# Two transformer blocks: sums of squares in two rounded parts, and the delta rule's first pair of heads prepared beside the gate projection

## The reference

```python
proj = hn @ w_in
qkv = silu(causal_conv(proj[..., :3 * 1024], w_conv))       # 4 taps, 24 heads' worth of 128 channels
gate = proj[..., 3 * 1024:4 * 1024]
q = l2_norm(q) * 128 ** -0.5;  k = l2_norm(k)               # over each head's 128 channels, 8 + 8 heads
g = -exp(a_log) * softplus(a_in + dt_bias)                  # decays; beta = sigmoid(b_in)
o = gated_delta_rule(q, k, v, g, beta)                      # chunked: a triangular solve per chunk, then a scan
o = rms_norm(o, norm_g) * silu(gate)
...
k = rms_norm(kv[:, :, 0], k_norm);  q = rms_norm(q, q_norm) # the later attention: 8 + 8 heads of 128
```

## Time and profile before

| | |
|---|---|
| three runs | 3090.63, 3101.42 and 3102.06 us, median 3101.42 |
| the profiled execution | 3092.16 us, span on the core 3090.2 us |
| PE busy | 2967.1 us, 96% of the span |
| DVE busy | 1464.2 us, 47% |
| ACT busy | 1074.8 us, 35% |
| POOL busy | 241.5 us, 8% |
| granted TensorE clock, mean | 0.986 of full |
| chain that ended last, share of PE | 81%, with L582 alone 64% |

### The profile page before, as it was taken

How to read it: one execution, slowest core, us unless ns; L and a number is a source line. 1 busy time by engine, 2 the same in 40 slices (tenths; PEclk the granted TensorE clock), 3 DMA queues, 4 the chain that set the end, 5 groups by cost and what they waited for, 6 DMA issues and landing times.

```text
span 3090.2 us, 46737 instructions
## 1 busy us (share of the span) xinstructions
PE 2967.1 (96%) x21198; PEld 2437.0 (79%) x21198; DVE 1464.2 (47%) x1427; ACT 1074.8 (35%) x1169; POOL 241.5 (8%) x136
## 2 busy tenths in 40 slices
PE   8998889999999999999999999999998998999998
PEld 6777767888877878888878887778877887788886
DVE  6655534444353444443354434455567664544432
ACT  4453333222254563222342223342244432232222
POOL 1002101000010001000110000330002211010001
PEclk9999889999999999999999999999999999999999
DMA  3210012222322102223222223312140002222221
GB/s 140 82 58 2 2 36 101 96 96 102 109 98 82 69 28 96 96 96 112 99 96 95 96 97 108 118 49 88 66 141 6 3 5 113 82 96 96 95 102 75
DMA packets 44901, 249.28 MB, mean 81 GB/s; under 512 B 8444, under 2 KB 12284, under 8 KB 17185
## 3 DMA queue, kind: packets, MB, share of 16 engines
q1 hardware_dynamic: 43552, 242.11, 22.1%
q10 hardware_dynamic: 1152, 4.19, 0.3%
HBM read 237.90 MB, written 8.39 MB: 80 GB/s over the span
## 4 chain that ended last, share of the span: by engine, by line
PE 81%; DVE 6%; ACT 3%; issue 2%; POOL 1%; DVEq 0%; ACTq 0%; POOLq 0%
PE ps L582 64%; PE ps L2672 7%; PE ps L1362 2%; PE ps L1990 1%; PE ps L2268 1%; ACT whi L266 1%; PE ps L2252 1%; DVE wlo L272 1%; PE ps L3705 1%; PE ps L3686 0%; PE ps L3717 0%; PE ps L3468 0%; DVE gdn_XX L1704 0%; PE ps L1422 0%; DVE rw_u L1035 0%
## 5 line engine op out<-in xcount | busy, mean ns | idle before, releaser
L272 DVE TENSOR_TENSOR wlo<-wraw,whi 128x2048 fp32r<-128x2048 f32 x210 | 486.6, 2317 | 987.8 <-ACT whi L266 987.7
L266 ACT ACTIVATE whi<-wraw 128x2048 fp32r<-128x2048 f32 x210 | 402.1, 1915 | 968.5 <-PE ps L582 968.4
L582 PE MATMUL ps<-ffn_xh,whi 128*128 128x512 f32 x1408 | 554.2, 394 | 3.6 <-DVE ffn_xl L389 2.1
L582 PE MATMUL ps<-ffn_xh,wlo 128*128 128x512 f32 x1408 | 550.0, 391 | 0.0
L582 PE MATMUL ps<-ffn_xl,whi 128*128 128x512 f32 x1408 | 549.3, 390 | 0.0
L582 PEld LDWEIGHTS ps<-ffn_xh,whi 128*128 128x128 f32 x1408 | 264.9, 188 | 61.1 <-DVE ffn_xl L389 2.5
L582 PEld LDWEIGHTS ps<-ffn_xh,wlo 128*128 128x128 f32 x1408 | 264.5, 188 | 59.2
L582 PEld LDWEIGHTS ps<-ffn_xl,whi 128*128 128x128 f32 x1408 | 264.7, 188 | 56.5 <-issue 0.7
L582 PE MATMUL ps<-ffn_uh,whi 128*128 128x512 f32 x704 | 276.6, 393 | 0.0
L582 PE MATMUL ps<-ffn_uh,wlo 128*128 128x512 f32 x704 | 274.9, 391 | 0.0
L582 PE MATMUL ps<-ffn_ul,whi 128*128 128x512 f32 x704 | 274.7, 390 | 0.0
(11 more groups left out here) (500 smaller groups left out, 4711.6 us busy)
## 6 DMA issues: line engine op xcount, KB each, us to landing
wraw<-in_weights SPq DMA_DIRECT2D x211, 1024.0 KB, 4.7
gates_kept<-gates_tmp ACTq DMA_DIRECT2D x8, 512.0 KB, 4.2
mix_gate<-gates_kept SPq DMA_DIRECT2D x8, 512.0 KB, 10.7
h<-in_x SPq DMA_DIRECT2D x4, 512.0 KB, 8.5
mix_y<-hz_kept SPq DMA_DIRECT2D x2, 1024.0 KB, 5.8
out<-out SPq DMA_DIRECT2D x4, 512.0 KB, 3.2
wraw<-in_weights SPq DMA_DIRECT2D x2, 512.0 KB, 6.9
ple_raw<-in_p SPq DMA_DIRECT2D x4, 256.0 KB, 5.1
```

Of the source, the lines that this page charges most:

```text
L266: c.nc.scalar.activation(c.whi[:, j % 2, :], c.wraw[:, j % 2, :], ACT.Copy).then_inc(c.hi_ready, 1)
L272: c.nc.vector.tensor_tensor(c.wlo[:, j % 2, :], c.wraw[:, j % 2, :], c.whi[:, j % 2, :].bitcast(F32), ALU.subtract).then_inc(c.lo_ready, 1)
L582: last = nc.tensor.matmul(pair[:, m, :], a, b, start=opens and n == 0 and wa + xa == 0, stop=closes and n == len(ks) - 1 and wa == 1)
```

## The change

Three things. First, each pair's squares are no longer summed as float32: ACT rounds them to float32r (`hi`), DVE subtracts (`lo`), and PE sums both parts, each as a float32r matmul; `Scales` and `HeadNorm` both do so, with single buffers `sq`, `hi`, `lo`. Second, in `gdn_qkv` the sum of pair p moves from its place after tile p + 3 to the middle of tile p + 2, and `Scales` comes ahead of `Decays` among the hooks of ACT and DVE. Third, stage -1 of `DeltaCore` is gone: the preparation of pair 0 is issued beside the gate projection's tiles 2 and 3, with buffers and PSUM banks of its own, and the zeroing of `XTf` moves into slot 2 of the first build. The lines of the attributes renamed by this (`self.KB` to `self.KB[p]` and the like) are left out below.

```diff
 class Scales
-        self.sq = [c.at(f"gdn_sq{b}", [P, 2, T], sq_at + 4096 * b) for b in range(4)]
+        self.sq, self.hi, self.lo = (c.at(f"gdn_sq{n}", [P, 2, T], sq_at + 4096 * b, dt)
+                                     for b, (n, dt) in enumerate((("", F32), ("h", F32R), ("l", F32R))))
-        self.hot = c.at("gdn_hot", [P, 2 * HEADS - 1], 20480)
+        self.hot = c.at("gdn_hot", [P, 2 * HEADS - 1], 20480, F32R)
...
     scalar_beside
             act.wait_ge(*self.qkv_part.A.at(f"gdn_qkv.func{p}"))
-            if p >= 4:
-                act.wait_ge(*self.E.at(f"sum{p - 4}"))
-            nc.scalar.activation(self.sq[p % 4][:, :, :], self.qkv[:, 2 * p:2 * p + 2, :], ACT.Square)\
+            if p:
+                act.wait_ge(*self.V.at(f"sqlo{p - 1}"))
+            nc.scalar.activation(self.sq[:, :, :], self.qkv[:, 2 * p:2 * p + 2, :], ACT.Square)\
                 .then_inc(*self.A.done(f"sq{p}"))
+            act.wait_ge(*self.A.at(f"sq{p}"))
+            if p:
+                act.wait_ge(*self.E.at(f"sum{p - 1}"))
+            nc.scalar.activation(self.hi[:, :, :], self.sq[:, :, :], ACT.Copy).then_inc(*self.A.done(f"sqhi{p}"))
...
     vector_beside
         if r == 1:
             nc.vector.memset(self.rows[:, :, :].bitcast(F32), 0.0).then_inc(*self.V.done("rows0"))
             nc.vector.memset(self.one[:, :].bitcast(F32), 0.0).then_inc(*self.V.done("one0"))
+        if 1 <= r <= 8:
+            p = r - 1
+            dve.wait_ge(*self.A.at(f"sqhi{p}"))
+            nc.vector.tensor_tensor(self.lo[:, :, :], self.sq[:, :, :], self.hi[:, :, :].bitcast(F32), ALU.subtract)\
+                .then_inc(*self.V.done(f"sqlo{p}"))
...
+    def tensor_halfway(self, pe, r):
+        nc, c = self.c.nc, self.c
+        if 2 <= r <= 9:
+            p = r - 2
+            pe.wait_ge(*self.V.at(f"sqlo{p}"))
+            for m in range(2):
+                h = 2 * (p % 4) + m
+                for part in (self.hi, self.lo):
+                    last = nc.tensor.matmul(c.ps[0:HEADS, 7 - p // 4, :], self.hot[:, HEADS - 1 - h:2 * HEADS - 1 - h],
+                                            part[:, m, :], start=h == 0 and part is self.hi,
+                                            stop=h == HEADS - 1 and part is self.lo)
+            last.then_inc(*self.E.done(f"sum{p}"))
...
     tensor_beside
-        if 3 <= r <= 10:
-            p = r - 3
-            pe.wait_ge(*self.A.at(f"sq{p}"))
-            pe.wait_ge(*self.V.at("hot"))
-            for m in range(2):
-                h = 2 * (p % 4) + m
-                last = nc.tensor.matmul(c.ps[0:HEADS, 7 - p // 4, :], self.hot[:, HEADS - 1 - h:2 * HEADS - 1 - h],
-                                        self.sq[p % 4][:, m, :], start=h == 0, stop=h == HEADS - 1)
-            last.then_inc(*self.E.done(f"sum{p}"))
 class DeltaCore
-        for s in range(-1, GP + 2):
+        for s in range(GP + 2):
...
     gpsimd
-        pool.wait_ge(self.c.tile_done, self.j_held)
         pool.wait_ge(self.loaded, 48)
         pool.wait_ge(*self.scales.V.at("cols"))
+        pool.wait_ge(*self.scales.A.at("low2"))
         self.pool_mask(pool, 0)
+        pool.wait_ge(self.c.tile_done, self.j_held)
...
     tensor
-        self.misc_read = None
-        pe.wait_ge(*self.scales.V.at("cols"))
-        pe.wait_ge(*self.scales.A.at("low2"))
+        self.misc_read = self.at("kb", 0)
+        pe.wait_ge(*self.gate_part.free(2))
+        pe.wait_ge(*self.gate_part.free(3))
...
+    def tensor_beside(self, pe, r):
+        if r == 2:
+            pe.wait_ge(*self.scales.A.at("low2"))
+            for s in (13, 15, 5):
+                self.pe_prepare(pe, 0, s)
+
+    def tensor_halfway(self, pe, r):
+        if r == 3:
+            pe.wait_ge(*self.scales.V.at("cols"))
+            self.pe_prepare(pe, 0, 7)
+            pe.wait_ge(*self.at("eg", 0))
+            self.pe_prepare(pe, 0, 9)
+            pe.wait_ge(*self.at("eg", 1))
+            self.pe_prepare(pe, 0, 11)
+
+    def single(self, p, s):
+        return self.bank({13: 4, 15: 5, 5: 7, 7: 6, 9: 4, 11: 5}[s] if p == 0 else self.MISC)
...
+    def scalar_early(self, act, r):
+        if r == 3:
+            self.c.nc.scalar.preload_act_table_set(LOG_EXP)
+            for s in (13, 15, 17):
+                self.act_prepare(act, 0, s)
...
+    def vector_beside(self, dve, r):
+        if r == 2:
+            dve.wait_ge(*self.scales.V.at("cols"))
+            for s in (13, 15, 16, 5, 7, 9, 11, 17):
+                self.dve_prepare(dve, 0, s)
...
     dve_build, slot 2
+            if k == 0:
+                nc.vector.memset(self.XTf[HALF:P, :, :, 0:HALF], 0.0).then_inc(*self.done("zero"))
 class HeadNorm
     scalar_beside
             if p:
+                act.wait_ge(*self.V.at(f"sqlo{p - 1}"))
+            nc.scalar.activation(self.sq[:, :, :], self.two(p), ACT.Square).then_inc(*self.A.done(f"sq{p}"))
+            act.wait_ge(*self.A.at(f"sq{p}"))
+            if p:
                 act.wait_ge(*self.E.at(f"sum{p - 1}"))
-            nc.scalar.activation(self.sq[:, :, :], self.two(p), ACT.Square).then_inc(*self.A.done(f"sq{p}"))
+            nc.scalar.activation(self.hi[:, :, :], self.sq[:, :, :], ACT.Copy).then_inc(*self.A.done(f"sqhi{p}"))
...
     vector_beside
+        if 0 <= s - 1 < 8:
+            p = s - 1
+            dve.wait_ge(*self.A.at(f"sqhi{p}"))
+            nc.vector.tensor_tensor(self.lo[:, :, :], self.sq[:, :, :], self.hi[:, :, :].bitcast(F32), ALU.subtract)\
+                .then_inc(*self.V.done(f"sqlo{p}"))
...
     tensor_beside
-            pe.wait_ge(*self.A.at(f"sq{p}"))
+            pe.wait_ge(*self.V.at(f"sqlo{p}"))
             if p:
                 pe.wait_ge(*self.A.at(f"log{p - 1}"))
             for m in range(2):
-                last = c.nc.tensor.matmul(c.ps[:, 6 + m, :], c.ones[:, :], self.sq[:, m, :], start=True, stop=True)
+                for part in (self.hi, self.lo):
+                    last = c.nc.tensor.matmul(c.ps[:, 6 + m, :], c.ones[:, :].bitcast(F32R), part[:, m, :], start=part is self.hi,
+                                              stop=part is self.lo)
 delta_stage
-    qkv_part.beside = qkv_part.beside_pe = (decays, scales)
+    qkv_part.beside, qkv_part.beside_pe, qkv_part.halfway = (scales, decays), (decays, scales), (scales,)
...
+    gate_part.beside = gate_part.beside_pe = (later, core)
+    gate_part.halfway = gate_part.early = (core,)
+    core.gate_part = gate_part
```

More of the change, by code:

```diff
@@ L1085, in __init__ @@
         self.E.plan([f"sum{p}" for p in range(8)] + ["cols"])
-        self.A.plan([f"sq{p}" for p in range(8)] + ["lq", "lk", "rq", "rk", "eG", "kd", "lkm"]
+        self.A.plan([f"{w}{p}" for p in range(8) for w in ("sq", "sqhi")] + ["lq", "lk", "rq", "rk", "eG", "kd", "lkm"]
                     + [f"one{n}" for n in range(3)] + [f"hi{x}" for x in range(3)]
                     + [f"{w}{x}" for x in range(3) for w in ("mid", "midrow")] + [f"low{x}" for x in range(3)] + ["egl"])
-        self.V.plan(["hot0", "hot", "rows0", "one0", "nd", "diag", "kdlog", "rkb", "cR"]
+        self.V.plan(["hot0", "hot", "rows0", "one0"] + [f"sqlo{p}" for p in range(8)] + ["nd", "diag", "kdlog", "rkb", "cR"]
                     + [f"rest{x}" for x in range(3)] + [f"last{x}" for x in range(3)] + ["cols"])
@@ L1365, in misc @@
     def misc(self, pe, read_by):
[L1367 to L1368 removed]
+        pe.wait_ge(*self.misc_read)
         self.misc_read = read_by
@@ L1421, in pe_build @@
                     t = slice(n * P, (n + 1) * P)
-                    last = nc.tensor.matmul(self.bank(self.Z_BANK + h)[:, t], self.k(k)[:, h, t], self.KB[:, h, t],
+                    last = nc.tensor.matmul(self.bank(self.Z_BANK + h)[:, t], self.k(k)[:, h, t], self.KB[k][:, h, t],
                                             start=True, stop=True)
@@ L1430, in pe_build @@
                     t = slice(n * P, (n + 1) * P)
-                    last = nc.tensor.matmul(self.bank(self.Z_BANK + h)[:, t], self.k(k)[:, h, t], self.Q1[:, h, t],
+                    last = nc.tensor.matmul(self.bank(self.Z_BANK + h)[:, t], self.k(k)[:, h, t], self.Q1[k][:, h, t],
                                             start=True, stop=True)
@@ L1502, in pe_prepare @@
             name, done = (("rb", "kb"), ("rq", "qn"), ("rg", "eg"))[what]
-            out = self.misc(pe, self.at(done, 2 * p + h))
+            out = self.misc(pe, self.at(done, 2 * p + h)) if p else self.single(p, s)
             i = 2 * p + h
@@ L1514, in pe_finish, with scalar_beside @@
                 .then_inc(*self.done("osum"))
+    def scalar_beside(self, act, r):
+        pass
+    def scalar_early(self, act, r):
[3 more added lines that the diff above has]
+                self.act_prepare(act, 0, s)
     def scalar(self, act):
@@ L1600, in act_prepare @@
                 act.wait_ge(*self.at("qd", p - 1))
-            nc.scalar.activation(self.eg[:, h, :], self.bank(self.MISC), ACT.Exp).then_inc(*self.done("eg"))
```

(16 more changed lines are left out.)

24 lines of the change are left out of this document (14 added, 10 removed).

## The result

The changed kernel takes 3146.68 us, median of four runs (3141.46 to 3147.10). Beside it the kernel before took 3098.04 us, median of four (3090.63 to 3102.06). The ratio is 1.0167, interval 1.0152 to 1.0181: slower, by 48.6 us. The forecast was 3136, the range 3117 to 3152. The profiled execution took 3147.1 us, its span is 3145.3 us, 55.1 more than before, at a mean granted clock of 0.975.

What follows compares the result with a forecast made beforehand. It took PE as the bound in qkv, but not between gate and first builds. 53.7 - 7.5 - 6.6 = +39.6 us on the profiled 3092.2 gave 3131.8; forecast 3136, range 3117 to 3152.

Steps and rivals of the forecast that it cites:

- The wait: In qkv tiles 2, 3 and 5 to 9, PE stands still some 7.1 us for DVE's subtraction, ready 12.6 us after the boundary.
- The clock: In qkv, PE restarts at half speed after each such gap, costing 1.6 us a gap.
- The rival in which the clock holds over gaps of 7 us: In qkv the gaps leave the clock up: +28 us, 3120; chance 0.10.
- the one in which it stays low until the tile ends: In qkv PE runs at half speed until each stalled tile ends: 3166 us; chance 0.06.
- Qkv in all: The qkv projection, tile by tile, becomes 53.7 us longer, cheaper sums included.
- The preparation of pair 0: Moved beside the gate projection, it saves a net 7.5 us, bounds 3 and 11.
- The wait for `low2`: Behind gate tile 2, PE waits 1.9 us; half of a 1.6 us clock loss is counted.
- `eg`: In the middle of gate tile 3, it is ready 1.2 us before PE asks, so its wait is hidden.
- `HeadNorm`: Beside the projections, eight sums fall from 1.74 to 0.92 us each: -6.6 us, bounds -6.6 and 0.

Runs made afterwards that it cites:

- only_qkv: Kernel before with only the qkv projection's sums changed (two rounded parts, middle of tile p + 2, ahead of the decays): 3148.59 us, ratio 1.0173.
- sum_later: Changed kernel with the sum of pair p in the middle of tile p + 3 instead of p + 2: 3081.71 us, ratio 0.9948 to the kernel before.
- decays_first: Changed kernel with Decays ahead of Scales again among the hooks of ACT and DVE: 3155.69 us, one run.
- filled: Changed kernel with 31 unused matmuls ahead of the wait in tiles 2, 3 and 5 to 9: 3132.01 us, ratio 1.0113.
- only_gate: Kernel before with only the first pair's preparation moved beside the gate projection: 3095.24 us, ratio 0.9995.
- sum_end: Changed kernel with the sum of pair p after the last matmul of tile p + 2 instead of in its middle: 3099.92 us, one run.
- after_busy: Changed kernel with eight extra matmuls in the sparse stretch of the recurrence: 3134.36 us, ratio 1.0131 to the kernel before.
- later_busy: sum_later with eight extra matmuls in the sparse stretch of the recurrence: 3072.00 us, ratio 0.9930 to the kernel before.
- only_headnorm: Kernel before with only the two rounded parts in HeadNorm: 3096.81 us, ratio 1.0004.
- before_busy: Kernel before with eight extra matmuls in the sparse stretch of the recurrence: 3093.42 us, ratio 0.9994.

## Why the prediction was right, point by point

**The wait.** This was the step that decided, and it held: 12.6 us from the boundary forecast, 12.4 to 12.5 measured; 7.1 us of standing still forecast, 6.8 to 6.9 measured; 8.7 in tile 2, measured 8.5; none in tile 4, as said. only_qkv shows that the loss is this part's, sum_later that it is the place's, decays_first that the pass is made of what I took it for.

**The clock.** 1.6 us a gap forecast, 1.85 measured by filled. A wait costs about the same whether it was 1.6, 3.0, 6.9 or 8.5 us long: eight, eight, nine and ten steps at 0.43 us. The rival in which the clock holds over gaps of 7 us, and the one in which it stays low until the tile ends, are both out.

**Qkv in all.** +53.7 forecast, 57.1 - 1.65 = +55.5 measured. A sum costs 0.92 us, as taken from the row with 128 columns.

**The preparation of pair 0.** -7.5 forecast, -7.0 measured in the change, -9.6 alone. The wait for `low2` is 1.6 us (1.9 forecast), and it lowered the clock for eight steps, 8 x 0.2 = 1.6 us, of which I had taken half. In only_gate that wait is 0.68 us and the clock stays at 1.00; these two, 0.9 and 1.6, are the 2.6 us between the two results. `eg` has 2.9 us of margin (1.2 forecast). The terms of the forecast add up to -7.3, not -7.5. That the forecast met the changed kernel so closely is partly luck, because the clock here falls in some executions and not in others. Seven profiled executions wait for `low2` at this place, each for 1.56 to 1.60 us; the clock fell within 2 us in five of them (the changed kernel, filled, sum_end, after_busy, later_busy) and not in two. One of the two is sum_later, PE's timeline and a window:

```profile
200.52 0.96 PE L1540 MATMUL ps<-gdn_rows,gdn_one 72*128 72x512 f32 x3 [1.60 <-ACT gdn_rows L1152]
```

```profile
200.00:204.00 4.00, 3.48 (x15) 2.90 (x16) 3.15 (x6) 3.93 (x5) 1.92 (x1) 1.00 0.13 53
```

The stretch from the end of qkv to behind `DeltaCore` gave -8.9 us there, -9.6 in only_gate, and only -4.4 in sum_end and in later_busy, where the granted clock was at half for 10 us more of that stretch than in sum_later.

**`HeadNorm`.** -6.6 forecast, -5.8 measured. The period beside the projections falls from 12.73 to 12.13 and 11.93 in turn, where I had 11.9 throughout; why every other tile keeps 0.2 us stays open.

**What the sum lacked.** Three parts add up to +39.6 by forecast and to 55.5 - 7.0 - 5.8 = +42.7 by the table, leaving out the opening, the recurrence and the -0.3 ahead of it. after_busy, which has no fall in the recurrence, says the same with runs: 3134.4 - 3092.7 = +41.7. The number on record, 3136, was 10.7 us too low, and the 3131.8 that the terms add up to was 15.3 under the profiled execution: 3.1 in the three parts, and 12.8, less 0.5 elsewhere, because the change lands on a program whose clock can fall elsewhere: 11.1 us in the recurrence and 1.65 in the opening. The opening is not the change's: after_busy, filled and decays_first have the same code there and lost at most 0.4 us. I had taken the base as fixed and read the 11 us between the runs of before as spread on either side; the 4.2 us that I put on top of 3131.8 stood for that spread. The range held the result because its upper end allowed for dearer gaps and for runs that fall high. The spread was one event of 11 us, absent from the profile that I read.

**What stays open.** The fall is in six profiled executions out of the nine without the added matmuls (the changed kernel, only_gate, only_headnorm, filled, sum_end, decays_first; not before, only_qkv, sum_later), and sum_later's other five runs, 7 to 13 us above its profiled one, suggest it there too. The kernel before seems to have it in only one run in four or five: 12 of its 55 runs lie over 3100. All of them share the instructions ahead of the stretch. Why versions that change code more than 1000 us earlier meet the fall more often was not found; that it depends on when the stretch comes, against something that runs on its own time, is a guess. The kept traces speak for it. In each of them all changes of the granted clock, falls and rises, lie on one evenly spaced raster, to 0.01 us. The point of that raster next behind the sparse stretch comes 43.3 to 43.5 us after the split that starts at 2308.97 in before, in all six executions with the fall, and 43.7 to 43.8 us after it in all three without. By the same count the profiled executions of after_busy and later_busy (43.4) would have had the fall, and that of before_busy (43.7) would not. No run moved the stretch on purpose, so this is a correlation in nine executions, and why the kernels differ in it stays open. So of the measured 48.6 us about 42 belong to the change by its own mechanism, and the rest to the clock's falls elsewhere, which the changed kernel's runs had more often than the runs beside them.

## What to carry to other kernels

Before moving a consumer ahead, count from the event that starts its producer's chain, and not from the consumer's old place: here the chain needed 12.5 us from the tile's end, the old place came 24 us after it, the new one 5.5, and the same place a tile later, 17.4 us, turned +42 into -21 us (both with the eight added matmuls). Where several runs of a kernel fall into two groups, one profile shows only one of them; find the stretch whose clock differs before you weigh a change of a few us against it. A few matmuls without use, in the sparsest stretch of a long small-matmul loop, can be worth more than the edit in hand: here 12.3 us on the changed kernel and 9.7 on sum_later, but 0.2 in the median of the kernel before, which rarely had the fall.

## What the runs showed of the hardware

- The clock of TensorE does not follow from the instruction stream alone. The same 4 us with PE busy for 1.91 are followed by 1.00 in one execution and by 0.56 and 0.50 in the next, for 27 us. So the sparse stretch has to be weighed as a chance.
- Short gaps can lower the clock, and with a delay. In the opening the gap in front of the norm's sum varies from run to run: in nine profiled executions it was 1.08 to 2.18 us and left the clock up, in three (the changed kernel, only_headnorm, sum_end) it was 2.35 to 2.74 us and did not; but at the gate 1.56 to 1.60 us was enough in five executions out of seven. PE's timeline of the changed kernel in the opening: the first float32r steps behind the gap are still quick, then come eight at 0.43 us.

```profile
26.14 1.12 PE L413 MATMUL ps<-norm_acc,ones 128*128 128x512 f32 x2 [2.35 <-POOL norm_acc L403]
...
27.34 0.40 PE L582 MATMUL ps<-gdn_xl,whi 128*128 128x512 f32 x1
27.57 0.59 PE L582 MATMUL ps<-gdn_xh,wlo 128*128 128x512 f32 x1
27.96 0.63 PE L582 MATMUL ps<-gdn_xh,whi 128*128 128x512 f32 x1
```

- In sum_end the clock held over a gap of 0.47 us and fell 0.9 us behind the one of 3.02 us. In all seven gaps of 6.8 us and more in the changed kernel it fell while PE still stood.
- Eight float32 matmuls of 128 columns, 2.3 us of PE in all, kept the clock up over the stretch in each profiled execution that had them, three of three; by the count under "What stays open", two of these would have lost it.
- A float32r matmul with eight weight columns takes as long as one with 128: 0.23 us for 512 columns of the moving side.
